# Attention values of two successive chunks in one group of matmuls on four 64x64 quarters of the array, and gate results on two PSUM banks

## The chip, the core and the metric

The kernel runs on one core of one Trainium2 chip. The metric is the device time of one execution in microseconds (us); before the change it is 826.69 us, the median of three runs (826.07 to 826.80). Five engines with instruction queues of their own work side by side: TensorE (PE, matrix products), VectorE (DVE), ScalarE (ACT), GpSimd (POOL) and SyncE (SP, here the queue that loads weights). They hand work over by semaphores. Matmul results go to PSUM, which has eight banks; the kernel uses them as pu0, pu1, pu2, ps0, ps1, pt, po and pc, each 128 partitions by 512 float32.

## The reference

Two layers of a hybrid encoder on 256 positions by 1024 channels, in float32. Per layer:

```
h = rmsnorm(x); proj = h @ w_in            # q | k | v | conv input | gate logits
q, k = rope(q), rope(k)
s = q_chunk . k_band / 8                   # chunks of 64; keys: previous chunk and own
m = max(max(s), sink); p = exp(s - m)
o = (p / (sum(p) + exp(sink - m))) @ v_band
y_attn = o @ w_attn_o
y_conv = silu(layernorm(dwconv31(glu(conv input)))) @ w_conv_o
x += (sigmoid(g_a) * y_attn + sigmoid(g_c) * y_conv) @ w_out
x += (silu(gt) * val) @ w_ffn_down         # gt, val = dwconv3(rmsnorm(x) @ w_ffn_up)
```

There are 16 query heads and 2 key/value heads of 64 channels, so 8 query heads share one key/value head; 4 chunks of 64 positions.

## The kernel before, in words

All activations lie with channels on partitions and the 256 positions along the free dimension. All weights are cut into units of 16 blocks of 128x128 (1 MB). Three slots hold raw weights; for unit u ACT rounds the raw block to a high part (`whi`, line 315) after TensorE has finished the unit that used the slot, GpSimd or VectorE subtracts for the low part (`wlo`, line 253), and TensorE forms each product from three matmuls (high times high, high times low, low times high, lines 1034 to 1036). A unit is 48 such matmuls. Slot and result bank of a unit are both u % 3. Before a unit overwrites its bank it waits until the unit three before it has been read (`result_read`).

Units per layer: 0 to 7 conv input, 8 keys and values, 9 to 12 queries, 13 to 20 gates (`U_GATE`), 21 to 24 attention output (`U_AO`), then conv output, merge output and the feed-forward units.

Attention is woven into the gate units. It has eight groups n (key/value head n // 4, chunk n % 4), each with 8 heads on four pairs. In iteration i TensorE runs gate unit U_GATE+i+1 (in the last iteration instead half of an attention output unit, `group_half(0, 0)`), then `transpose_probs(i)` (line 1157, into bank pt), then `values(i-1)` (line 1168, into the first half of po). Scores of two groups at a time (line 1146) are put into the middle of every second gate unit; they already run as 64x64 matmuls. After the last iteration come `group_half(1, 0)`, `values(7)`, the channel sums of the convolution (`sum_quarters`, line 1064, bank ps0), and `group_half(0, 1)`, which needs all groups. Float32 matmuls such as the transposes, the scores and the values appear as two records for each one in the program.

In `values(n)` the two matmuls have all 128 keys on the rows of the array and 64 of its columns each: even heads go to partitions 0 to 63 of the output, odd heads to 64 to 127. They wait for the copy of the transposed probabilities, and for the reading of the output of the group before (`ol_ready`), as there is one output bank.

ACT in iteration i: copy the transposed probabilities of i-1 (`evict_transposed`, line 478), exponentials of i (`exps`, line 493), high part of the attention output of i-2 (`high_of_o`, line 484, semaphore `oh_ready`), scale the probabilities of i (`probabilities`, line 502), tanh of gate unit i (line 516), `whi` of the unit three later (line 315), and two products for the convolution (line 343). DVE in iteration i: maxima, convolution taps, denominators (lines 808, 812), low part of the attention output of i-2 (`low_of_o`, line 818, semaphore `ol_ready`), more taps. The order on each engine is the written order of the code; no scheduler changes it.

Of the kernel before, what the change touches and what calls it, by code (L numbers as in the profile page):

```python
# [9 lines left out]
P = 128  # L10
# [64 lines left out]
def hybrid_encoder(nc, x_in, pos_in, const_in, par_in, gf_in, w_in, y_out):  # L75
# [3 lines left out]
    with ctx:  # L79
# [62 lines left out]
        outputs = po[:, 0, :].rearrange("p (b t) -> p b t", b=GROUP_PAIRS)  # L142
# [24 lines left out]
        tr_done, pt_ready, pv_done, oh_ready, ol_ready = sem("tr_done"), sem("pt_ready"), sem("pv_done"), sem("oh_ready"), sem("ol_ready")  # L167
        xc_ready, t_ready, silu_ready, uh_ready, ul_ready = sem("xc_ready"), sem("t_ready"), sem("silu_ready"), sem("uh_ready"), sem("ul_ready")
# [17 lines left out]
        def lo_count(s, n):  # L186

            return n + PIECES

# [117 lines left out]
        def _(act):  # L307
# [103 lines left out]
            for l in range(DEPTH):  # L411
# [68 lines left out]
                def high_of_o(n):  # L480

                    c, g = n % N_CHUNKS, n // N_CHUNKS
                    act.wait_ge(pv_done, l * GROUPS + n + 1)
                    A(oh[:, 4 * g:4 * g + 4, CHUNK * c:CHUNK * c + CHUNK], outputs, ACT.Copy).then_inc(oh_ready, 1)
# [20 lines left out]
                for i in range(NT):  # L505
                    u = U_GATE + i
                    if i >= 1:
                        evict_transposed(i - 1)
                    exps(i)
                    if i >= 2:  # L510
                        high_of_o(i - 2)
                    probabilities(i)
                    if i == 4:
                        act.wait_ge(rope_done, l * 10 + 10)
                    act.wait_ge(unit_done[u % RING], finished(l, u))
                    A(gate[:, :, i, :], pu[u % RING][:, :, :], ACT.Tanh, scale=0.5).then_inc(gate_ready, 1)
                    next_high(l, u)
# [24 lines left out]
                for i in range(4):  # L542
                    act.wait_ge(m_step, l * 12 + 4 + 2 * i + 2)
                    A(hh[:, 2 * i:2 * i + 2, :], pu[(U_CO + i) % RING][:, :, :], ACT.Copy, scale=0.5).then_inc(hh_ready, 1)
                    next_high(l, U_CO + i)
                for i in range(4):
                    act.wait_ge(x_ready, l * 8 + i + 1)
                    y = pu[(U_OUT + i) % RING]
# [76 lines left out]
        def _(dve):  # L625
# [94 lines left out]
            for l in range(DEPTH):  # L720
# [93 lines left out]
                def low_of_o(n):  # L814
                    c, g = n % N_CHUNKS, n // N_CHUNKS
                    dve.wait_ge(oh_ready, l * GROUPS + n + 1)
                    at = (slice(0, P), slice(4 * g, 4 * g + 4), slice(CHUNK * c, CHUNK * c + CHUNK))
                    V.tensor_tensor(ol[at], outputs, oh[at].bitcast(f32), ALU.subtract).then_inc(ol_ready, 1)
# [16 lines left out]
                def merge_attention(i):  # L835

                    u = U_AO + i
                    dve.wait_ge(gate_ready, l * NT + NT)
                    dve.wait_ge(unit_done[u % RING], finished(l, u))
                    g0 = gate[:, 0, 2 * i:2 * i + 2, :]  # L840
                    V.scalar_tensor_tensor(g0, g0, 1.0, pu[u % RING][:, :, :], ALU.add, ALU.mult).then_inc(m_step, 1)
# [38 lines left out]
                for i in range(4):  # L880
                    u = U_CO + i
                    dve.wait_ge(unit_done[u % RING], finished(l, u))
                    dve.wait_ge(m_step, l * 12 + 4 + 2 * i)
                    y = pu[u % RING][:, :, :]
# [13 lines left out]
                def input_low(i):  # L898

                    y = pu[(U_OUT + i) % RING]  # L900
# [20 lines left out]
                for i in range(4):  # L921
# [3 lines left out]
                    V.tensor_tensor(pu[u % RING][:, :, :], pu[u % RING][:, :, :], x2, ALU.add).then_inc(x_ready, 1)  # L925
# [9 lines left out]
                    V.tensor_copy(x2, pu[u % RING][:, :, :]).then_inc(x_copied, 1)  # L935
                dve.wait_ge(rstd_ready, l * 3 + 3)

                def scale_up(s, ab, done_value):

                    dve.wait_ge(unit_done[s], done_value)  # L940
                    V.tensor_tensor(up[:, ab, :, :], pu[s][:, :, :], rstd[:, :].unsqueeze(1).to_broadcast([P, 2, T]),  # L941
                                    ALU.mult).then_inc(up_ready, 1)
# [24 lines left out]
                scale_up(0, 0, finished(l, U_FFN))  # L967
                hidden_tile(k0, 0, PA_FW, PA_FW + FT * 4)
                split_low(0, 12)
                scale_up(1, 1, finished(l, U_FFN + 1))  # L970
# [4 lines left out]
                def ffn_step(j, parity, last):  # L975
                    k = j * 2 + l * FT
                    col = j * 8 + PA_FW
                    scale_up(2, 0, l * USES + j + 11)
# [3 lines left out]
                    scale_up(0, 1, l * USES + j + 12)  # L982
# [44 lines left out]
        def _(pe):  # L1027
# [10 lines left out]
            def unit(s, uses_before, hi, lo, ready=None, between={}):  # L1038
# [3 lines left out]
                for m in range(2):  # L1042
                    for k in range(NT):
# [4 lines left out]
                        last = product(pu[s][:, m, :], s, 2 * k + m, hi[:, k, :], lo[:, k, :], k == 0, k == NT - 1)  # L1048
# [28 lines left out]
            def paired_unit(s, hi, lo, before, sums):  # L1077

                for p in range(NT // 2):
                    before(p)  # L1080
                    for k in (2 * p, 2 * p + 1):
                        for m in range(2):
                            last = product(pu[s][:, m, :], s, 2 * k + m, hi[:, k, :], lo[:, k, :], k == 0 and m == 0, k == NT - 1, True)
# [31 lines left out]
            for l in range(DEPTH):  # L1115
                def standard(u, hi, lo, ready=None, between={}):
                    if u >= RING:
                        pe.wait_ge(*result_read(l, u - RING))
                    unit(u % RING, uses(l, u), hi, lo, ready, between)

                def in_pairs(u, hi, lo, ready):
# [4 lines left out]
                    paired_unit(s, hi, lo, ready, {})  # L1126
# [33 lines left out]
                def values(n):  # L1160
                    c, g = n % N_CHUNKS, n // N_CHUNKS
                    pe.wait_ge(v_ready, l * 2 + 2)
                    pe.wait_ge(pt_ready, l * GROUPS + n + 1)
                    if n:
                        pe.wait_ge(ol_ready, l * GROUPS + n)
                    for odd in range(2):
                        rows, queries = slice(64 * odd, 64 * odd + 64), slice(CHUNK * (odd ^ (n % 2)), CHUNK * (odd ^ (n % 2)) + CHUNK)
                        last = MM(outputs[rows, :, :], vwin[:, c, HEAD_DIM * g:HEAD_DIM * g + HEAD_DIM],
                                  probsT[n % 2][:, :, queries], start=True, stop=True)
                    last.then_inc(pv_done, 1)  # L1170
# [22 lines left out]
                else:  # L1193
                    for s in range(UNSCALED):
                        pe.wait_ge(hi_ready[s], hi_count(l * USES))
                        pe.wait_ge(lo_ready[s], lo_count(s, l * USES))
                        paired_unit(s, uh, ul, unscaled_parts, {1: first_total} if s == 1 else {})
# [8 lines left out]
                if l == 0:  # L1206
                    pe.wait_ge(*result_read(l, U_GLU))
                    pe.wait_ge(hi_ready[0], hi_count(1))
                    paired_unit(0, hh, hl, fourth_parts, {})
# [19 lines left out]
                def group_half(i, group):  # L1229

                    s, n = (U_AO + i) % RING, uses(l, U_AO + i)
                    if group == 0:
                        pe.wait_ge(*result_read(l, U_AO + i - RING))
# [3 lines left out]
                        pe.wait_ge(ol_ready, l * GROUPS + N_CHUNKS)  # L1237
# [3 lines left out]
                    for m in range(2):  # L1241
                        for k in range(GROUP_PAIRS * group, GROUP_PAIRS * (group + 1)):
                            last = product(pu[s][:, m, :], s, 2 * k + m, oh[:, k, :], ol[:, k, :],
# [57 lines left out]
                def ffn_step(j, parity):  # L1301
# [3 lines left out]
                    unit(2, n + 10, uh, ul)  # L1305
                    pe.wait_ge(up_ready, k)
                    unit(0, n + 11, uh, ul)
# [97 lines left out]
```

## Time and profile before

| what | value |
|---|---|
| median of 3 runs | 826.69 us |
| the profiled execution, its own time | 827.24 us |
| span of its trace | 825.44 us |
| TensorE busy | 808.1 us, 98% of the span |
| VectorE, ScalarE, GpSimd busy | 71%, 63%, 55% |
| granted TensorE clock | 0.997 of full speed |
| all values matmuls (line 1168) | 64 records, 10.4 us |
| all transposes of probabilities (line 1157) | 64 records, 9.7 us |
| all scores (line 1146) | 256 records, 8.8 and 2.7 us |

A record on TensorE reaches from its start to the modelled end of its results; records overlap, so the cost of a step is read from start to start. A line of the timeline merges neighbouring records of one kind: its second number is the time from the first start to the last end. The iterations described above lie at about 95 to 159 us (first layer) and 496 to 560 us (second layer).

### The profile page before, as it was taken

How to read it: one execution, taken by the hardware profiler on the slowest of the kernel's cores; microseconds unless marked ns; L12 is line 12 of the kernel's file. 1: busy time of each engine (PE TensorE's matmuls, PEld its weight loads, DVE VectorE, ACT ScalarE, POOL GpSimd, SP SyncE). 2: the span in 40 equal slices, each digit the busy share in tenths (PEclk: the TensorE clock that was granted, in tenths of full speed). 3: DMA queues.
4: the chain of work that ended last, by engine and by line, in shares of the span. 5: the costliest groups of instructions: out<-in, count | busy, mean ns of one | idle time of the engine just before them, and what ended most of it. 6: DMA issues, size and time to landing. Idle time of an engine off the chain costs nothing.

```text
span 825.4 us, 16620 instructions
## 1 busy us (share of the span) xinstructions
PE 808.1 (98%) x6820; PEld 790.5 (96%) x6820; DVE 588.8 (71%) x1162; ACT 518.8 (63%) x852; POOL 456.7 (55%) x140
## 2 busy tenths in 40 slices
PE   8999999999999999999999999999999999999996
PEld 7999989899999999999999999989999999999995
DVE  5799998583559766666579999876535887665664
ACT  6856798773665655555576587887446654554543
POOL 6898787687722233222289987887875032223220
PEclk9999999999999999999999999999999999999998
DMA  8654444445455655555455544444454456545521
GB/s 288 212 204 148 161 151 150 154 155 189 169 172 185 205 187 177 199 170 188 154 197 168 198 154 154 154 145 151 165 194 165 157 202 204 202 155 201 179 81 52
DMA packets 21386, 142.26 MB, mean 172 GB/s; under 512 B 2624, under 2 KB 3136, under 8 KB 4672
## 3 DMA queue, kind: packets, MB, share of 16 engines
q1 hardware_dynamic: 20592, 140.43, 49.5%
q8 instruction: 54, 0.88, 0.4%
q10 hardware_dynamic: 720, 0.78, 0.3%
q14 instruction: 20, 0.16, 0.1%
HBM read 140.15 MB, written 1.05 MB: 171 GB/s over the span
## 4 chain that ended last, share of the span: by engine, by line
PE 78%; ACT 9%; DVE 8%; issue 2%; DMA 1%; POOL 1%; SPq 0%; DVEq 0%; ACTq 0%
PE pu L1034 21%; PE pu L1035 20%; PE pu L1036 20%; ACT whi L315 4%; DVE wlo L894 3%; PE ps L1034 2%; PE ps L1036 2%; PE ps L1035 2%; DVE pc L749 2%; ACT qk L563 1%; PE pt L1036 1%; PE pt L1035 1%; PE pt L1034 1%; DMA x<-in_x_t 1%; DVE gate L941 1%
## 5 line engine op out<-in xcount | busy, mean ns | idle before, releaser
L253 POOL TENSOR_TENSOR wlo<-raw,whi 128x2048 fp32r<-128x2048 f32 x86 | 397.3, 4624 | 334.0 <-ACT whi L315 333.8
L1034 PE MATMUL pu<-uh,whi 128*128 128x256 f32 x880 | 249.8, 284 | 1.8 <-POOL wlo L253 1.4
L315 ACT ACTIVATE whi<-raw 128x2048 fp32r<-128x2048 f32 x129 | 245.7, 1906 | 8.3 <-PE pu L1036 7.3
L1035 PE MATMUL pu<-ul,whi 128*128 128x256 f32 x880 | 249.0, 283 | 0.0
L1036 PE MATMUL pu<-uh,wlo 128*128 128x256 f32 x880 | 249.0, 283 | 0.0
L1034 PE MATMUL pu<-hh,whi 128*128 128x256 f32 x704 | 201.6, 286 | 2.2 <-POOL wlo L253 1.4
L1035 PE MATMUL pu<-hl,whi 128*128 128x256 f32 x704 | 199.1, 283 | 0.0
L1036 PE MATMUL pu<-hh,wlo 128*128 128x256 f32 x704 | 199.1, 283 | 0.0
L1034 PEld LDWEIGHTS pu<-uh,whi 128*128 128x128 f32 x880 | 168.9, 192 | 2.4 <-issue 2.3
L1035 PEld LDWEIGHTS pu<-ul,whi 128*128 128x128 f32 x880 | 168.9, 192 | 0.1
L1036 PEld LDWEIGHTS pu<-uh,wlo 128*128 128x128 f32 x880 | 168.9, 192 | 0.0
L749 DVE SCALAR_TENSOR_TENSOR pc<-upad,par_all,pc 128x256 f32<-128x256 f32 x404 | 162.9, 481 | 0.1
L1034 PEld LDWEIGHTS pu<-hh,whi 128*128 128x128 f32 x704 | 134.9, 192 | 8.2 <-issue 7.1
L1035 PEld LDWEIGHTS pu<-hl,whi 128*128 128x128 f32 x704 | 135.0, 192 | 0.0
L1036 PEld LDWEIGHTS pu<-hh,wlo 128*128 128x128 f32 x704 | 135.0, 192 | 0.0
L563 ACT ACTIVATE qk<-gate,par_all 128x256 f32<-128x256 f32 x88 | 48.2, 594 | 124.7 <-DVE gate L941 124.7
L894 DVE TENSOR_TENSOR wlo<-raw,whi 128x2048 fp32r<-128x2048 f32 x42 | 95.9, 2284 | 0.0
L955 DVE SCALAR_TENSOR_TENSOR qk<-gate,par_all,qk 128x254 f32<-128x254 f32 (+1 forms) x176 | 73.3, 478 | 30.0 <-ACT qk L563 30.0
L941 DVE TENSOR_TENSOR gate<-pu,rstd 128x512 f32<-128x512 f32 x44 | 30.2, 687 | 63.9 <-PE pu L1036 57.4
L1034 PE MATMUL ps<-oh,whi 128*128 128x256 f32 x176 | 50.0, 284 | 0.5 <-DVE ol L963 0.5
L1036 PE MATMUL ps<-oh,wlo 128*128 128x256 f32 x176 | 49.8, 283 | 0.0
L1035 PE MATMUL ps<-ol,whi 128*128 128x256 f32 x176 | 49.8, 283 | 0.0
(210 smaller groups left out, 1232.9 us busy)
## 6 DMA issues: line engine op xcount, KB each, us to landing
raw<-in_weights SPq DMA_DIRECT2D x130, 1024.0 KB, 4.9
raw<-in_weights SPq DMA_DIRECT2D x3, 512.0 KB, 8.8
x<-in_x_t SPq DMA_DIRECT2D x2, 256.0 KB, 4.8
raw<-in_weights SPq DMA_DIRECT2D x2, 256.0 KB, 3.9
x<-in_x_t SPq DMA_DIRECT2D x1, 512.0 KB, 8.0
out_y<-qk SPq DMA_DIRECT2D x2, 256.0 KB, 2.8
out_y<-qk ACTq DMA_DIRECT2D x2, 256.0 KB, 2.7
par_all<-in_params SPq DMA_DIRECT2D x1, 236.0 KB, 6.9
```

The lines of the kernel that those rows point to most:

```text
L253: nc.gpsimd.tensor_tensor(wlo[s][:, :], raw[s][:, :], whi[s][:, :].bitcast(f32), ALU.subtract).then_inc(lo_ready[s], 1)
L315: A(whi[s][:, :], raw[s][:, :], ACT.Copy).then_inc(hi_ready[s], 1)
L563: A(fbuf[:, ab, half, :], up[:, ab, half, :], ACT.Identity, scale=par[:, col + 2:col + 2 + 1], bias=par[:, col + 3:col + 3 + 1]).then_inc( ...
L749: V.scalar_tensor_tensor(out, upad[:, t, k:k + T], w, sums, ALU.mult, ALU.add).then_inc(conv_step, 1)
L894: V.tensor_tensor(wlo[s][:, :], raw[s][:, :], whi[s][:, :].bitcast(f32), ALU.subtract).then_inc(lo_ready[s], 1)
L941: V.tensor_tensor(up[:, ab, :, :], pu[s][:, :, :], rstd[:, :].unsqueeze(1).to_broadcast([P, 2, T]), ALU.mult).then_inc(up_ready, 1)
L955: last = V.scalar_tensor_tensor(acc, up[:, ab, half, 0:T - shift], par[:, col:col + 1], acc, ALU.mult, ALU.add).then_inc(f_tap, 1)
L1034: MM(out, whi[s][:, w], hi, start=start, stop=False, skip_group_check=accumulate)
L1035: MM(out, whi[s][:, w], lo, start=False, stop=False, skip_group_check=accumulate)
L1036: return MM(out, wlo[s][:, w], hi, start=False, stop=stop, skip_group_check=accumulate)
```

## The change

- `values` is called for two groups at once, n and n+1, in iterations 2, 4 and 6 (before the transposes of that iteration) and once after the loop. It issues eight matmuls of 64 rows by 64 columns in two turns. In the first turn group n uses one half of the keys and group n+1 the other half, so that four matmuls stand on four quarters; in the second turn the halves are exchanged and the results are added to those of the first. Between the turns TensorE waits for its own semaphore `first_keys`.
- Even groups write po, odd groups pu0 (the last one pu2).
- To free pu0, gate results go to pu1 and pu2 in turn, so a gate unit waits for the reading of the unit two before it. Weight slots stay u % 3. From unit 21 up to the second feed-forward unit the banks are named in the order 1, 0, 2.
- The high and low parts of the attention output lag by three iterations; iteration 7 handles group 4 and 5, the end groups 6 and 7.

```diff
+        def result_bank(u):
+            if U_GATE <= u < U_AO:
+                return 1 + (u - U_GATE) % 2
+            return (1, 0, 2)[u % RING] if U_AO <= u < U_FFN + 2 else u % RING
+        def used_before(u):
+            return u - 2 if U_GATE + 2 <= u <= U_AO else u - RING
...
-                    if i >= 2:
+                    if i >= 3:
+                        high_of_o(i - 3)
+                    if i == GROUPS - 1:
                         high_of_o(i - 2)
...
-                    if i >= 2:
+                    if i >= 3:
+                        low_of_o(i - 3)
+                    if i == GROUPS - 1:
                         low_of_o(i - 2)
...
                 def values(n):
-                    c, g = n % N_CHUNKS, n // N_CHUNKS
+                    g = n // N_CHUNKS
                     pe.wait_ge(v_ready, l * 2 + 2)
-                    pe.wait_ge(pt_ready, l * GROUPS + n + 1)
+                    pe.wait_ge(pt_ready, l * GROUPS + n + 2)
                     if n:
                         pe.wait_ge(ol_ready, l * GROUPS + n)
-                    for odd in range(2):
-                        rows, queries = slice(64 * odd, 64 * odd + 64), slice(CHUNK * (odd ^ (n % 2)), CHUNK * (odd ^ (n % 2)) + CHUNK)
-                        last = MM(outputs[rows, :, :], vwin[:, c, HEAD_DIM * g:HEAD_DIM * g + HEAD_DIM],
-                                  probsT[n % 2][:, :, queries], start=True, stop=True)
-                    last.then_inc(pv_done, 1)
+                    if n == GROUPS - 2:
+                        pe.wait_ge(gate_ready, l * NT + NT)
+                    for turn in range(2):
+                        if turn:
+                            pe.wait_ge(first_keys, l * (GROUPS // 2) + n // 2 + 1)
+                        for m in (n, n + 1):
+                            c = m % N_CHUNKS
+                            keys = slice(64 * (turn ^ (m % 2)), 64 * (turn ^ (m % 2)) + 64)
+                            for odd in range(2):
+                                rows, queries = slice(64 * odd, 64 * odd + 64), slice(CHUNK * (odd ^ (m % 2)), CHUNK * (odd ^ (m % 2)) + CHUNK)
+                                last = MM(outputs(m)[rows, :, :], vwin[keys, c, HEAD_DIM * g:HEAD_DIM * g + HEAD_DIM],
+                                          probsT[m % 2][keys, :, queries], start=(turn == 0), stop=(turn == 1), skip_group_check=True)
+                        last.then_inc(*((pv_done, 2) if turn else (first_keys, 1)))
...
-                        pe.wait_ge(ol_ready, l * GROUPS + N_CHUNKS)
+                        pe.wait_ge(ol_ready, l * GROUPS + N_CHUNKS + 2 * i)
...
+                    if i and i % 2 == 0:
+                        values(i - 2)
                     transpose_probs(i)
-                    if i:
-                        values(i - 1)
                 group_half(1, 0)
-                values(GROUPS - 1)
+                values(GROUPS - 2)
```

On TensorE in iteration 2 of the first layer, before (pt: transposed probabilities, po: attention output, pu: unit results; the number of slot or bank stands behind a name):

```order
L1036 MATMUL pu1<-hh,wlo1 128x256
L1157 MATMUL pt<-const,probs0 128x128 [waits pt_ready,rope_done,p_ready]
L1157 MATMUL pt<-const,probs0 128x128 x3
L1168 MATMUL po<-probsT1,vwin 64x256 [waits ol_ready,pt_ready,v_ready]
L1168 MATMUL po<-probsT1,vwin 64x256
L1034 MATMUL pu2<-hh,whi2 128x256 [waits lo_ready2,hi_ready2,gate_ready]
```

The same place now:

```order
L1054 MATMUL pu2<-hh,wlo1 128x256
L1194 MATMUL po<-probsT0,vwin 64x256 [waits pt_ready,v_ready]
L1194 MATMUL po<-probsT0,vwin 64x256
L1194 MATMUL pu0<-probsT1,vwin 64x256 x2
L1194 MATMUL po<-probsT0,vwin 64x256 [waits first_keys]
L1194 MATMUL po<-probsT0,vwin 64x256
L1194 MATMUL pu0<-probsT1,vwin 64x256 x2
L1175 MATMUL pt<-const,probs0 128x128 [waits pt_ready,rope_done,p_ready]
L1175 MATMUL pt<-const,probs0 128x128 x3
L1052 MATMUL pu1<-hh,whi2 128x256 [waits lo_ready2,hi_ready2,gate_ready]
```

The values of groups 0 and 1 now stand ahead of the transposes of group 2; before, the values of group 0 stood one unit earlier and those of group 1 behind these transposes.

On TensorE after the last iteration, between the two halves of the attention output units, before:

```order
L1036 MATMUL pu1<-oh,wlo1 128x256
L1168 MATMUL po<-probsT1,vwin 64x256 [waits ol_ready,pt_ready,v_ready]
L1168 MATMUL po<-probsT1,vwin 64x256
L1064 MATMUL ps0<-cv,quarter 32x256 [waits conv_step,pool_conv,exp_done]
L1064 MATMUL ps0<-cv,quarter 32x256 x3
L1064 MATMUL ps0<-cv,quarter 32x256 [waits conv_step]
L1064 MATMUL ps0<-cv,quarter 32x256 x3
L1034 MATMUL pu0<-oh,whi0 128x256 [waits ol_ready,oh_ready]
```

The same place now:

```order
L1054 MATMUL pu0<-oh,wlo1 128x256
L1194 MATMUL po<-probsT0,vwin 64x256 [waits ol_ready,gate_ready,pt_ready,v_ready]
L1194 MATMUL po<-probsT0,vwin 64x256
L1194 MATMUL pu2<-probsT1,vwin 64x256 x2
L1194 MATMUL po<-probsT0,vwin 64x256 [waits first_keys]
L1194 MATMUL po<-probsT0,vwin 64x256
L1194 MATMUL pu2<-probsT1,vwin 64x256 x2
L1082 MATMUL ps0<-cv,quarter 32x256 [waits conv_step,pool_conv,exp_done]
L1082 MATMUL ps0<-cv,quarter 32x256 x3
L1082 MATMUL ps0<-cv,quarter 32x256 [waits conv_step]
L1082 MATMUL ps0<-cv,quarter 32x256 x3
L1052 MATMUL pu1<-oh,whi0 128x256 [waits ol_ready,oh_ready]
```

Values of two groups stand here where there was one; before, the values of group 6 stood one half unit earlier.

On ACT in the last iteration and behind it, now (line 492 copies transposed probabilities, 507 are the exponentials, 498 the high part of the attention output, 516 the scaling, 532 the tanh, 380 the copy of the channel sums):

```order
L492 ACTIVATE probsT<-pt 128x512 [waits tr_done]
L505 ACTIVATE mass<-mass 128x4 [waits mx_step]
L507 ACTIVATE probs,mass<-ps,less_top 128x128 x4
L498 ACTIVATE oh<-po 128x4x64 [waits pv_done]
L498 ACTIVATE oh<-pu 128x4x64 [waits pv_done]
L516 ACTIVATE probs<-probs,share 128x128 [waits den_step]
L516 ACTIVATE probs<-probs,share 128x128 x3
L532 ACTIVATE gate<-pu 128x2x256 [waits unit_done2]
L329 ACTIVATE whi<-raw 128x2048 [waits unit_done2,raw_in2]
L492 ACTIVATE probsT<-pt 128x512 [waits tr_done]
L498 ACTIVATE oh<-po 128x4x64 [waits pv_done]
L498 ACTIVATE oh<-pu 128x4x64 [waits pv_done]
```

Before, one high part (of group 5) stood between the exponentials and the scaling; the rest of the row is as it was.

## Rows read from the trace of the kernel before

**Rows 1.** The page: busy time of the engines; the chain that ended last

```profile
PE 808.1 (98%) x6820; PEld 790.5 (96%) x6820; DVE 588.8 (71%) x1162; ACT 518.8 (63%) x852; POOL 456.7 (55%) x140
...
PE 78%; ACT 9%; DVE 8%; issue 2%; DMA 1%; POOL 1%; SPq 0%; DVEq 0%; ACTq 0%
```

**Rows 2.** Timeline of TensorE, iteration 0: start, length, line, operation, [idle before]

```profile
101.73 0.66 PE L1157 MATMUL pt<-const,probs 128*128 128x128 f32 x4 [0.16 <-ACT probs L502]
102.14 0.36 PE L1034 MATMUL pu<-hh,whi 128*128 128x256 f32 x1
102.34 0.28 PE L1035 MATMUL pu<-hl,whi 128*128 128x256 f32 x1
```

**Rows 3.** Timeline of TensorE, iteration 1, with values of group 0

```profile
110.74 0.28 PE L1036 MATMUL pu<-hh,wlo 128*128 128x256 f32 x1
110.86 0.60 PE L1157 MATMUL pt<-const,probs 128*128 128x128 f32 x4
111.39 0.65 PE L1168 MATMUL po<-probsT,vwin 128*64 128x256 f32 x4
111.98 0.38 PE L1034 MATMUL pu<-hh,whi 128*128 128x256 f32 x1
112.20 0.28 PE L1035 MATMUL pu<-hl,whi 128*128 128x256 f32 x1
```

**Rows 4.** Line 1168 on TensorE: shortest, median, longest record in ns

```profile
L1168 PE MATMUL po<-probsT,vwin x64: 379/404/430, 111.4 to 558.4; 128*64 128x256 f32 x64
```

**Rows 5.** Timeline of TensorE, scores on four quarters, in iterations 1 and 3

```profile
106.86 1.10 PE L1146 MATMUL ps<-kr,qk 64*64 64x128 f32 x32 [1.62 <-ACT probs L493]
...
121.80 0.28 PE L1036 MATMUL pu<-hh,wlo 128*128 128x256 f32 x1
122.01 1.10 PE L1146 MATMUL ps<-kr,qk 64*64 64x64 f32 x32
```

**Rows 6.** Timeline of ACT, iterations 0, 2 and 3: tanh, weights, tanh, last exponential

```profile
101.58 0.58 ACT L516 ACTIVATE gate<-pu 128x512 f32<-128x512 f32 x1
102.06 1.90 ACT L315 ACTIVATE whi<-raw 128x2048 fp32r<-128x2048 f32 x1
...
115.40 0.58 ACT L516 ACTIVATE gate<-pu 128x512 f32<-128x512 f32 x1
...
120.34 0.22 ACT L493 ACTIVATION_READ_ACCUMULATOR probs<-ps,less_top 128x1 f32 x1
```

**Rows 7.** Timeline of TensorE, iterations 6 and 7 and the end, first layer

```profile
148.12 0.60 PE L1157 MATMUL pt<-const,probs 128*128 128x128 f32 x4
...
152.82 0.66 PE L1157 MATMUL pt<-const,probs 128*128 128x128 f32 x4 [0.45 <-ACT probs L502]
...
157.05 0.65 PE L1168 MATMUL po<-probsT,vwin 128*64 128x256 f32 x4
157.63 1.07 PE L1064 MATMUL ps<-cv,quarter 128*32 128x256 f32 x16
158.73 0.36 PE L1034 MATMUL pu<-oh,whi 128*128 128x256 f32 x1
```

**Rows 8.** Timeline of ACT, iteration 7 and the end, first layer

```profile
148.99 0.58 ACT L478 ACTIVATE probsT<-pt 128x512 f32<-128x512 f32 x1
...
150.93 0.39 ACT L484 ACTIVATE oh<-po 128x256 fp32r<-128x256 f32 x1
151.49 1.28 ACT L502 ACTIVATE probs<-probs,share 128x128 f32<-128x128 f32 x4 [0.17 <-DVE share L812]
...
157.75 0.38 ACT L484 ACTIVATE oh<-po 128x256 fp32r<-128x256 f32 x1 [1.94 <-PE po L1168]
```

**Rows 9.** Timeline of DVE, the low part of the last group

```profile
158.16 0.42 DVE L818 TENSOR_TENSOR ol<-po,oh 128x256 fp32r<-128x256 f32 x1 [1.90 <-ACT oh L484]
```

**Rows 10.** Timeline of TensorE, the same two places of the second layer

```profile
553.85 0.66 PE L1157 MATMUL pt<-const,probs 128*128 128x128 f32 x4 [0.45 <-ACT probs L502]
...
559.77 0.36 PE L1034 MATMUL pu<-oh,whi 128*128 128x256 f32 x1
```

More of the change, by code:

```diff
@@ L141, in hybrid_encoder, with outputs @@
         fold = [h32[:, n, :] for n in range(2)]
-        outputs = po[:, 0, :].rearrange("p (b t) -> p b t", b=GROUP_PAIRS)
+        def outputs(n):
+            into = po if n % 2 == 0 else pu[2] if n == GROUPS - 1 else pu[0]
+            return into[:, 0, :].rearrange("p (b t) -> p b t", b=GROUP_PAIRS)
         raw_in = [sem(f"raw_in{s}") for s in range(RING)]
@@ L167, in hybrid_encoder @@
         tr_done, pt_ready, pv_done, oh_ready, ol_ready = sem("tr_done"), sem("pt_ready"), sem("pv_done"), sem("oh_ready"), sem("ol_ready")
+        first_keys = sem("first_keys")
         xc_ready, t_ready, silu_ready, uh_ready, ul_ready = sem("xc_ready"), sem("t_ready"), sem("silu_ready"), sem("uh_ready"), sem("ul_ready")
@@ L483, in high_of_o @@
                     act.wait_ge(pv_done, l * GROUPS + n + 1)
-                    A(oh[:, 4 * g:4 * g + 4, CHUNK * c:CHUNK * c + CHUNK], outputs, ACT.Copy).then_inc(oh_ready, 1)
+                    A(oh[:, 4 * g:4 * g + 4, CHUNK * c:CHUNK * c + CHUNK], outputs(n), ACT.Copy).then_inc(oh_ready, 1)
                 def exps(n):
@@ L515, in _ @@
                     act.wait_ge(unit_done[u % RING], finished(l, u))
-                    A(gate[:, :, i, :], pu[u % RING][:, :, :], ACT.Tanh, scale=0.5).then_inc(gate_ready, 1)
+                    A(gate[:, :, i, :], pu[result_bank(u)][:, :, :], ACT.Tanh, scale=0.5).then_inc(gate_ready, 1)
                     next_high(l, u)
@@ L543, in _ @@
                     act.wait_ge(m_step, l * 12 + 4 + 2 * i + 2)
-                    A(hh[:, 2 * i:2 * i + 2, :], pu[(U_CO + i) % RING][:, :, :], ACT.Copy, scale=0.5).then_inc(hh_ready, 1)
+                    A(hh[:, 2 * i:2 * i + 2, :], pu[result_bank(U_CO + i)][:, :, :], ACT.Copy, scale=0.5).then_inc(hh_ready, 1)
                     next_high(l, U_CO + i)
@@ L840, in merge_attention @@
                     g0 = gate[:, 0, 2 * i:2 * i + 2, :]
-                    V.scalar_tensor_tensor(g0, g0, 1.0, pu[u % RING][:, :, :], ALU.add, ALU.mult).then_inc(m_step, 1)
+                    V.scalar_tensor_tensor(g0, g0, 1.0, pu[result_bank(u)][:, :, :], ALU.add, ALU.mult).then_inc(m_step, 1)
                 assert step_now == CONV_STEPS
@@ L924, in _ @@
                     x2 = x[:, 2 * i:2 * i + 2, :]
-                    V.tensor_tensor(pu[u % RING][:, :, :], pu[u % RING][:, :, :], x2, ALU.add).then_inc(x_ready, 1)
+                    V.tensor_tensor(pu[result_bank(u)][:, :, :], pu[result_bank(u)][:, :, :], x2, ALU.add).then_inc(x_ready, 1)
                     if i >= 2:
@@ L1036, in product, with unit @@
                 return MM(out, wlo[s][:, w], hi, start=False, stop=stop, skip_group_check=accumulate)
-            def unit(s, uses_before, hi, lo, ready=None, between={}):
+            def unit(s, into, uses_before, hi, lo, ready=None, between={}):
                 pe.wait_ge(hi_ready[s], hi_count(uses_before))
@@ L1047, in unit @@
                             ready(k // 2)
-                        last = product(pu[s][:, m, :], s, 2 * k + m, hi[:, k, :], lo[:, k, :], k == 0, k == NT - 1)
+                        last = product(pu[into][:, m, :], s, 2 * k + m, hi[:, k, :], lo[:, k, :], k == 0, k == NT - 1)
                 last.then_inc(unit_done[s], 1)
@@ L1075, in _, with paired_unit @@
             pe.wait_ge(setup, 3)
-            def paired_unit(s, hi, lo, before, sums):
+            def paired_unit(s, into, hi, lo, before, sums):
                 for p in range(NT // 2):
@@ L1082, in paired_unit @@
                         for m in range(2):
-                            last = product(pu[s][:, m, :], s, 2 * k + m, hi[:, k, :], lo[:, k, :], k == 0 and m == 0, k == NT - 1, True)
+                            last = product(pu[into][:, m, :], s, 2 * k + m, hi[:, k, :], lo[:, k, :], k == 0 and m == 0, k == NT - 1, True)
                     if p == NT // 2 - 1:
@@ L1117, in standard @@
                     if u >= RING:
-                        pe.wait_ge(*result_read(l, u - RING))
-                    unit(u % RING, uses(l, u), hi, lo, ready, between)
+                        pe.wait_ge(*result_read(l, used_before(u)))
+                    unit(u % RING, result_bank(u), uses(l, u), hi, lo, ready, between)
                 def in_pairs(u, hi, lo, ready):
@@ L1125, in in_pairs @@
                     pe.wait_ge(lo_ready[s], lo_count(s, n))
-                    paired_unit(s, hi, lo, ready, {})
+                    paired_unit(s, result_bank(u), hi, lo, ready, {})
                 def parts_ready(high, high_before, low, low_before):
@@ L1242, in group_half @@
                         for k in range(GROUP_PAIRS * group, GROUP_PAIRS * (group + 1)):
-                            last = product(pu[s][:, m, :], s, 2 * k + m, oh[:, k, :], ol[:, k, :],
+                            last = product(pu[result_bank(U_AO + i)][:, m, :], s, 2 * k + m, oh[:, k, :], ol[:, k, :],
                                            k == 0 and m == 0, k == NT - 1, True)
@@ L1304, in ffn_step @@
                     pe.wait_ge(up_ready, k - 1)
-                    unit(2, n + 10, uh, ul)
+                    unit(2, 2, n + 10, uh, ul)
                     pe.wait_ge(up_ready, k)
-                    unit(0, n + 11, uh, ul)
+                    unit(0, 0, n + 11, uh, ul)
                     pe.wait_ge(hi_ready[1], hi_count(n + 11))
```

28 lines of the change are left out of this document (14 added, 14 removed).

## The prediction

> **What bounds the kernel now.** I read the page first: TensorE is busy for 98% of the span and holds most of the chain that ended last [rows 1]. Whatever is started later or takes longer on TensorE's queue is therefore nearly all paid, and work on ACT and DVE counts only where TensorE waits for it. Next I read TensorE's timeline through the attention iterations. It shows matmul after matmul 0.12 us apart and three places where another engine decides: the scores in iteration 1 of the first layer (idle 1.62 us for the exponentials [rows 5]), the transposes of group 7 (idle 0.45 us for the scaled probabilities [rows 7], again in the second layer [rows 10]), and the half unit at 158.73, which waits for the low part that DVE ends at 158.16 + 0.42 = 158.58 [rows 7, 9]. The last two lie just where the change moves things.
>
> **What one group of values costs now.** Start to start: transposes at 110.86, the second matmul of the next unit at 112.20, so 1.34 us with values [rows 3]. Without values it is 102.34 - 101.73 = 0.61, of which 0.06 is the first transpose, longer there because it had waited (0.66 for 0.60) [rows 2, 3]; so 0.55. One group costs 1.34 - 0.55 = 0.78. Of that 0.58 is the block itself (111.39 to 111.98), the rest is the change from 128x128 to 64-column matmuls and back, 0.10 on either side. Sixteen groups are 12.5 us.
>
> **What a pair will cost.** The records of one group start within 0.65 - 0.38 = 0.27 us, and the last one takes 0.38 until its results stand [rows 3, 4]. Is a quarter matmul cheaper? A float32 record of 128 columns goes through in 0.11 us in the transposes (three further starts in 0.60 - 0.27). The scores are 32 records of 64x128 in 1.10 us [rows 5]: one at a time they would take 3.5 us, in fours 8 x 0.11 plus 0.16 until the last results (a transpose record is 0.60 - 3 x 0.11 = 0.27 long, of which 0.11 is the stream) and a first load of 0.05 (430 less 379 ns [rows 4]), which is 1.10. So four quarters work at once, but each record needs as long as a full one. Half the rows and twice the matmuls then leave the streaming time as it was: two turns of 2 x 0.22 us for a pair, two groups of 2 x 0.22 before. Nothing is won there.
> - First turn: 0.65, plus 0.02 for four quarters instead of two, until its results stand.
> - The wait on `first_keys`: nothing hides it, since the whole queue of TensorE stands behind it. The trace has no wait of TensorE on itself. From below it is a turn that flows on; from above the 0.15 between DVE's end at 158.58 and the matmul at 158.73. TensorE to ACT takes 0.05 (157.05 + 0.65 to 157.75 [rows 7, 8]). I take 0.06, nearest to that single hand-over.
> - Second turn, to the next start: 0.58.
> - Entry from a 128x128 unit: 0.21 (121.80 to 122.01 [rows 5]) instead of 0.12, so 0.09; the first transpose behind it 0.06.
>
> The block is 0.67 + 0.06 + 0.59 = 1.32, the pair 1.47 against 1.56 for two groups. The mode changes saved are nearly eaten by letting the array run empty between the turns.
>
> The Trainium skill, TensorEngine Tiling (Array Packing), section Instruction Overhead, gives each matmul some 60 cycles of overhead, which speaks against twice as many. By its figure the 8 extra records of a pair would add 0.2 us (an estimate at 2.4 GHz), some 1.6 us in all. The scores bear it out only partly: their records start in fours in 0.11 us, the streaming time.
>
> **Two banks for gates.** A gate unit now needs the tanh of the unit two before it. The first to wait is at 102.14, its tanh ends at 101.58 + 0.58 = 102.16 [rows 2, 6]: up to 0.1 us, and free in the first layer, since TensorE idles 1.62 us for ACT afterwards. Later the tanh of iteration 2 ends at 115.98, while its unit starts about 24 x 0.12 before the scores at 122.01, at 118.9: 2.9 us of slack. The exponentials that scores need end at 120.56 [rows 6]; they come 0.6 later (below), the scores 0.1 earlier, and 0.7 us of slack is left. Cost 0.
>
> **Where the path goes, first layer, as shift against before.**
> 1. Transposes of group 6. Before them stood five groups, 3.9 us; now three pairs, 4.4 us. Shift +0.48 at their end. (Each pair stands ahead of the transposes of its iteration, which is also why ACT is late by 0.6 in iterations 3 and 5.)
> 2. Their copy on ACT started at 148.99 though they ended at 148.72, as ACT was busy. It now starts at 148.72 + 0.48 + 0.06 = 149.27: +0.28.
> 3. Between exponentials and scaling stand two high parts instead of one. The second costs about 0.30 to the next start (0.38, less the 0.09 by which ACT records overlap, 102.06 against 102.16 [rows 6]); of the 0.56 from 150.93 to 151.49, 0.17 was a wait for DVE [rows 8], which it covers, and 0.60 now stands for 0.56. Scaling, and with it the transposes of group 7: +0.32. TensorE idles for it as before, longer.
> 4. The values of group 6 are gone from behind them: -0.78, shift -0.46 at the last values. The copy of group 7 is ready by then: tanh, weights and copy after the scaling end by 156, the pair starts at 156.6.
> 5. Pair instead of one group: 1.32 against 0.58, shift +0.28 at the channel sums.
> 6. The half unit behind waits for two high parts in a row on ACT before the last low part: +0.30. Shift +0.58.
>
> Behind that point order and durations are unchanged and TensorE leads, so nothing gives it back. The second layer shows the same idle time before the transposes of group 7, and from them to the half unit 5.92 us against 5.91 [rows 7, 10], so the same sum is taken for it. Two layers: +1.2 us. GpSimd, DMA and later bank names: 0; their work starts from the same units, shifted by less than a microsecond.
>
> The profiled execution is 827.24 (span 825.44 and 1.8 around it), so it would be 828.4; it lies 0.55 above the median of 826.69. From the median: 827.8 us.
>
> **Rivals.**
> - *The turns flow on without running empty.* For it: a second turn needs only weights and data that are long there. Against: weight loads of the second turn stand behind the wait. A pair is then 0.28 cheaper (0.23 of wait and latency, 0.05 of first load): 1.19. Transposes of group 6 shift by -0.35, ACT by -0.6 to -0.5, and each layer ends near -0.6: 825.5 us.
> - *Slower by the starts.* Not the stream but the start of each quarter matmul decides. The 32 records of the scores allow up to 1.10 / 32 = 0.034 us each [rows 5]; 8 more in each pair are 0.27, counted four times a layer (three ahead of group 6, one at the end): +2.2, 830.0 us. Decisive if four quarters with 256 columns start more than 0.22 us after the four before.
> - *Slower, since the two row halves take turns.* Values of both halves are read and added in two banks; if only two quarters ran at once, a pair would take four blocks of streaming, +0.85, four times a layer: +6.8, 834.6 us. Against: 1.10 us for the scores. It decides from the point where the first turn lasts over 0.9 us.
> - *The end is not longer.* If the second high part and the third pair hide in ACT's slack (steps 2, 3 and 6 nothing), each layer is at about 0: 826.7 us.
>
> **How the numbers follow.** Main case 0.68, own range 827.0 to 828.7 (wait of 0 to 0.15 beyond the results; steps 3 and 6 half or full). Flowing turns 0.13; starts 0.07; row halves 0.05; no longer end 0.07. A measurement here tells 0.2%, or 1.65 us, from no change: below 825.04 is faster, above 828.34 slower. Main case 0.53 same, 0.15 slower; flowing turns 0.06 same, 0.07 faster; starts and row halves 0.12 slower; the last 0.07 same. Together faster 0.07, same 0.66, slower 0.27. The range for 8 in 10 takes in most of the flowing and of the starts case: 825.5 to 830.0.
>
> **What would show it.** Right: the first turn's records start within 0.28 us, the second turn starts 0.45 us after the last of the first, and a block lasts 1.3 us; the transposes of group 7 start 0.3 us later against a fixed point of the layer, with some 1.1 us of idle before them (0.45, 0.32 for ACT, 0.30 since the values of group 5 no longer lie between); the half unit after the channel sums waits for DVE's low part about 0.3 us longer. Wrong: a block near 1.1 or above 1.6 us, a gate unit that waits for a tanh for more than 0.2 us in many iterations, or a TensorE wait on GpSimd that was not there.

## The result, and the profile after

The changed kernel takes 828.19 us (median of 11 runs, 827.83 to 829.79) against 826.59 us for the kernel before (11 runs, 826.07 to 827.15): ratio 1.0021, 95% interval 1.0013 to 1.0029. The forecast was 827.8 us, "same" at 0.66, with 828.34 as the edge to slower. It is slower by 1.6 us, and the interval lies clear of no change; the median stays under the edge, so it counts as "same".

The page of the profiled execution (828.07 us, span 826.3) answers to [rows 1]; TensorE's busy time is even a little less than before, and the granted clock is 0.998 of full speed against 0.997, so the clock is not behind the difference:

```profile
PE 807.4 (98%) x6884; PEld 791.0 (96%) x6884; DVE 588.7 (71%) x1162; ACT 518.9 (63%) x852; POOL 456.7 (55%) x140
```

The list of TensorE's waits (line that waited, line it waited for, total us, times, longest) shows where time went. The second line was 1.1 us in total before; the waits for `ol L834` (DVE's low part of the attention output) were not there:

```profile
PE pu L1052 <- POOL wlo L267: 2.9, 3, 1.4
PE pt L1175 <- ACT probs L516: 2.2, 3, 1.0
PE ps L1164 <- ACT probs L507: 1.5, 1, 1.5
...
PE pu L1052 <- DVE ol L834: 0.8, 2, 0.4
```

Two groups of values in eight matmuls are called a pair here; its block is the time from its first start to the start of the next kind of matmul. Now the first pair on TensorE's timeline (start, length, line), which answers to [rows 3]:

```profile
116.32 0.28 PE L1054 MATMUL pu<-hh,wlo 128*128 128x256 f32 x1
116.53 0.43 PE L1194 MATMUL po<-probsT,vwin 64*64 64x256 f32 x2
116.54 0.43 PE L1194 MATMUL pu<-probsT,vwin 64*64 64x256 f32 x2
116.79 0.38 PE L1194 MATMUL po<-probsT,vwin 64*64 64x256 f32 x2
116.81 0.38 PE L1194 MATMUL pu<-probsT,vwin 64*64 64x256 f32 x2
117.28 0.43 PE L1194 MATMUL po<-probsT,vwin 64*64 64x256 f32 x2
117.29 0.43 PE L1194 MATMUL pu<-probsT,vwin 64*64 64x256 f32 x2
117.54 0.38 PE L1194 MATMUL po<-probsT,vwin 64*64 64x256 f32 x2
117.56 0.38 PE L1194 MATMUL pu<-probsT,vwin 64*64 64x256 f32 x2
117.87 0.66 PE L1175 MATMUL pt<-const,probs 128*128 128x128 f32 x4
```

Four quarters start within 0.02 us, their second records 0.26 later; then nothing starts until 117.28, because the second turn waits for the first turn's results, which the profile puts at 116.81 + 0.38 = 117.19 (the ends of matmuls are modelled there, the starts are not). The block from 116.53 to 117.87 is 1.34 us for two groups, where one group took 0.58.

TensorE at the end of the first layer's attention part, answering to [rows 7]:

```profile
148.03 0.66 PE L1175 MATMUL pt<-const,probs 128*128 128x128 f32 x4
...
152.59 0.66 PE L1175 MATMUL pt<-const,probs 128*128 128x128 f32 x4 [1.04 <-ACT probs L516]
...
157.39 1.07 PE L1082 MATMUL ps<-cv,quarter 128*32 128x256 f32 x16
158.84 0.36 PE L1052 MATMUL pu<-oh,whi 128*128 128x256 f32 x1 [0.38 <-DVE ol L834]
```

and ACT at the same places, answering to [rows 8]:

```profile
148.72 0.60 ACT L492 ACTIVATE probsT<-pt 128x512 f32<-128x512 f32 x1 [0.39 <-PE pt L1175]
...
150.69 0.40 ACT L498 ACTIVATE oh<-po 128x256 fp32r<-128x256 f32 x1
150.95 0.41 ACT L498 ACTIVATE oh<-pu 128x256 fp32r<-128x256 f32 x1
151.25 1.28 ACT L516 ACTIVATE probs<-probs,share 128x128 f32<-128x128 f32 x4
...
157.53 0.38 ACT L498 ACTIVATE oh<-po 128x256 fp32r<-128x256 f32 x1 [2.23 <-PE pu L1194]
157.81 0.38 ACT L498 ACTIVATE oh<-pu 128x256 fp32r<-128x256 f32 x1
```

The low part of the last group on DVE, answering to [rows 9], ends at 158.28 + 0.41 = 158.69, and the half unit starts at 158.84:

```profile
158.28 0.41 DVE L834 TENSOR_TENSOR ol<-pu,oh 128x256 fp32r<-128x256 f32 x1
```

Two executions differ in how early the first inputs are there (here 0.63 us, to the other side; over all profiled runs the same scores start between 105.54 and 106.86), so starts are best compared from a fixed point of each layer. I take the start of the scores in iteration 1, which stand ahead of the first pair: 106.86 and 507.89 before, 106.23 and 508.01 after.

```profile
106.23 1.10 PE L1164 MATMUL ps<-kr,qk 64*64 64x128 f32 x32 [1.52 <-ACT probs L507]
```

From there, in us (first layer; the second agrees within 0.03 in these two kernels and in all of the experiments but the last):

| kernel | transposes of group 6 | transposes of group 7 | channel sums | half unit behind the sums |
|---|---|---|---|---|
| before | 41.26 | 45.96 | 50.77 | 51.87 |
| changed | 41.80 | 46.36 | 51.16 | 52.61 |

A layer is 0.74 us longer at the half unit (0.72 in the second); 1.46 us in all, of the 1.6 measured. Behind that point the starts run in step again: 229.12 against 229.01 for the same matmul at the head of the second feed-forward unit, which is 0.63 earlier at the fixed point and 0.74 later since.

### The profile page after: what moved, and what is told of

Same layout as the page of the kernel before. It is cut to its first block, busy times and chain, and to the rows that moved or that the text cites. A ratio compares the mean times of both kernels' runs of the same rounds, so it can differ in the third digit from the quotient of the medians.

```text
span 826.3 us, 16742 instructions
## 1 busy us (share of the span) xinstructions
PE 807.4 (98%) x6884; PEld 791.0 (96%) x6884; DVE 588.7 (71%) x1162; ACT 518.9 (63%) x852; POOL 456.7 (55%) x140
## 4 chain that ended last, share of the span: by engine, by line
PE 79%; DVE 8%; ACT 8%; issue 2%; DMA 1%; POOL 1%; SPq 0%; DVEq 0%; ACTq 0%
PE pu L1052 21%; PE pu L1054 21%; PE pu L1053 21%; ACT whi L329 3%; DVE wlo L912 3%; PE ps L1052 2%; PE ps L1053 2%; PE ps L1054 2%; DVE pc L765 2%; PE po L1194 1%; ACT qk L579 1%; PE pt L1054 1%; PE pt L1053 1%; PE pt L1052 1%; PE pt L1175 1%
```

## The experiments

They were timed in two sessions, each beside the kernel before on the same chip (before: 826.37 us in the session of the first four, 826.24 in that of the last three). Each kernel ran 11 times, the last one 5 times. The table gathers what came out; the last two columns are starts from the fixed point as above, the half unit being the one behind the channel sums.

| kernel | median us | ratio to before, 95% interval | block | transposes 7 | half unit |
|---|---|---|---|---|---|
| full rows, one turn | 825.09 | 0.9984 (0.9975 to 0.9993) | 1.015 | 45.37 | 51.28 |
| banks only | 826.20 | 0.9998 (0.9989 to 1.0007) | 0.582 (one group) | 45.98 | 51.90 |
| turns flow on | 825.93 | 0.9994 (0.9986 to 1.0003) | 1.025 | 45.41 | 51.36 |
| other end | 827.39 | 1.0013 (1.0004 to 1.0021) | 1.343 | 46.34 | 52.33 |
| full rows and other end | 824.54 | 0.9979 (0.9970 to 0.9987) | 1.015 | 45.38 | 51.03 |
| and third buffer | 824.30 | 0.9976 (0.9967 to 0.9985) | 1.014 | 45.27 | 50.92 |
| and late products | 823.60 | 0.9966 (0.9954 to 0.9979) | 1.014 | 44.41 | 50.58 |

### Full rows, one turn

```diff
-                    for turn in range(2):
-                        if turn:
-                            pe.wait_ge(first_keys, ...)
-                        for m in (n, n + 1):
...
+                    for m in (n, n + 1):
+                        c = m % N_CHUNKS
+                        for odd in range(2):
+                            rows, queries = ...
+                            last = MM(outputs(m)[rows, :, :], vwin[:, c, HEAD_DIM * g:HEAD_DIM * g + HEAD_DIM],
+                                      probsT[m % 2][:, :, queries], start=True, stop=True)
+                    last.then_inc(pv_done, 2)
```

> The changed kernel with one thing undone: the values of a pair run in one turn as four matmuls of 128 rows by 64 columns (group n into po, group n+1 into the second bank), with no halves of the keys and no wait on first_keys; pairing, order and gate banks stay. If the price is the emptying of the array between the turns and quarters win nothing in streaming, a block takes 1.00 us from its first start to the next kind of matmul (0.27 + 2 x 0.21 + 0.31) instead of 1.34, the transposes of group 7 come 0.65 earlier than in the kernel before (ACT leads there), and the half unit behind the channel sums 0.6 to 0.7 earlier: two layers -1.3, some 825.3 us, 0.16% below before and 2.9 us below the changed kernel. If pairing itself (later copies, two high parts in a row) is what costs, it stays at or above 826.6 us.

TensorE's timeline at the first pair:

```profile
115.83 0.65 PE L1190 MATMUL po<-probsT,vwin 128*64 128x256 f32 x4
116.31 0.60 PE L1190 MATMUL pu<-probsT,vwin 128*64 128x256 f32 x4
116.84 0.66 PE L1175 MATMUL pt<-const,probs 128*128 128x128 f32 x4
```

The second group starts 0.48 us after the first, with nothing between. The block is 1.01 us instead of 1.34, the time 825.09, where 825.3 was expected. Undoing the quarters, and with them the wait between the turns, turns a loss of 1.6 us into a gain of 1.3 against before. So pairing is worth something, and the quarters with their wait cost more than it. The other theory, that pairing itself is the loss, falls.

### Banks only

```diff
-            into = po if n % 2 == 0 else pu[2] if n == GROUPS - 1 else pu[0]
+            into = po
...
-                    if i and i % 2 == 0:
-                        values(i - 2)
                     transpose_probs(i)
+                    if i:
+                        values(i - 1)
```

`values`, the high and low parts and the end are those of the kernel before.

> The kernel before with the bank part alone: gate results on pu1 and pu2 in turn, banks 1, 0, 2 behind; values one group at a time as before. If two banks are enough for the gates, nothing moves: 826.6 us, TensorE's starts through the attention iterations as before within 0.1 us, apart from at most 0.1 us at the gate unit of iteration 1, which the idle time before the scores takes up. If the narrower banks are behind the part of the loss that was not forecast (0.15 us a layer), it shows 0.15 us or more a layer by the first transposes of group 7.

The transposes of group 7 wait as they did:

```profile
152.39 0.66 PE L1171 MATMUL pt<-const,probs 128*128 128x128 f32 x4 [0.46 <-ACT probs L516]
```

From the fixed point on, starts agree with the kernel before within 0.03 us. Two banks are enough for the gates; the 0.16 us a layer that the forecast missed is not here.

### Turns flow on

```diff
-                        if turn:
-                            pe.wait_ge(first_keys, ...)
...
-                                last = MM(outputs(m)[rows, :, :], ..., start=(turn == 0), stop=(turn == 1), skip_group_check=True)
-                        last.then_inc(*((pv_done, 2) if turn else (first_keys, 1)))
+                                last = MM(outputs(m ^ turn, turn)[rows, :, :], ..., start=True, stop=True)
+                    last.then_inc(pv_done, 2)
```

`outputs(n, half)` takes the second half of the bank where `half` is 1.

> The changed kernel with the second turn written to the second halves of the same two banks, each bank by the same half of the rows as in the first turn, so that TensorE needs no wait between the turns. The addition of the second turn's results is left out, so part of the attention output is missing. Everything else is as in the changed kernel. If the wait costs what the trace shows (0.46 us from the last start of the first turn to the second turn, against 0.21 in a flow, and a first load of 0.05), a block takes 1.04 us and the time is near 825.6 us (-1.0 against before). If quarters have a cost of their own besides the wait, the block stays above 1.15 us.

```profile
116.48 0.43 PE L1192 MATMUL po<-probsT,vwin 64*64 64x256 f32 x2
116.49 0.43 PE L1192 MATMUL pu<-probsT,vwin 64*64 64x256 f32 x2
116.74 0.38 PE L1192 MATMUL po<-probsT,vwin 64*64 64x256 f32 x2
116.76 0.38 PE L1192 MATMUL pu<-probsT,vwin 64*64 64x256 f32 x2
116.96 0.38 PE L1192 MATMUL po<-probsT,vwin 64*64 64x256 f32 x2
116.97 0.38 PE L1192 MATMUL pu<-probsT,vwin 64*64 64x256 f32 x2
117.18 0.38 PE L1192 MATMUL po<-probsT,vwin 64*64 64x256 f32 x2
117.19 0.38 PE L1192 MATMUL pu<-probsT,vwin 64*64 64x256 f32 x2
117.50 0.66 PE L1175 MATMUL pt<-const,probs 128*128 128x128 f32 x4
```

Without the wait the second set of four starts 0.26 us after the first, as in the changed kernel, and each further set follows after 0.22 us; the block is 1.025 us. The wait thus costs 1.343 - 1.025 = 0.318 us a pair, and quarters as such cost 0.010 over full rows. In the trace the half unit comes 0.51 and 0.53 earlier than before in the two layers; the timed runs show less of it (-0.4 us, interval from -1.2 to +0.2). Part of that difference lies outside the kernel's instructions: the median span of these executions is 823.7 us against 824.6 before, 0.9 less, but in six of the eleven 2.2 to 2.5 us passed outside the span instead of the usual 1.8. No run shows why. The price of the wait rests on the traces. Part of the result is left out here, so this is not a version to use: the second halves would have to be added afterwards.

### Other end

```diff
+                    if i == GROUPS - 1:
+                        evict_transposed(i)
                     next_high(l, u)
-                evict_transposed(GROUPS - 1)
...
                     for m in range(2):
+                        if m and (i, group) == (1, 0):
+                            values(GROUPS - 2)
...
                 group_half(1, 0)
-                values(GROUPS - 2)
```

> The changed kernel with another end of the attention part: ACT copies the transposed probabilities of group 7 before the weights instead of after, and the last pair stands in the middle of the half unit behind the transposes of group 7, so the high and low parts of groups 6 and 7 lie beside its second half. If the idle time before the last half unit (0.38 us in the trace of the changed kernel) is the two high parts in a row, it is gone, the channel sums come 0.3 later for one more change of mode, and each layer is 0.2 to 0.3 us shorter: about 827.7 us. If the half unit waits there for something else, the idle time stays.

```profile
157.12 0.28 PE L1055 MATMUL pu<-oh,wlo 128*128 128x256 f32 x1
157.33 1.07 PE L1083 MATMUL ps<-cv,quarter 128*32 128x256 f32 x16
158.33 0.39 PE L1053 MATMUL pu<-oh,whi 128*128 128x256 f32 x1
```

The half unit behind the sums now follows them without idle time (0.31 us from the last of them instead of 0.76), the sums stand 0.17 later for the further change of mode, and a layer is 0.28 shorter than in the changed kernel. So the idle time was the two high parts in a row on ACT, with DVE behind them: it is gone once they lie beside matmuls.

### Full rows and other end

The two edits above together.

> The two edits that each helped, together: pairs in one turn on all 128 rows, and the other end (copy of group 7 ahead of the weights, last pair in the middle of the half unit). The first took 0.60 us out of each layer against the kernel before, the second 0.27 against the changed kernel. If they add up, each layer is 0.87 shorter than before: 1.7 us, some 824.7 us. If the wait of the transposes of group 7 for ACT (1.2 us idle) takes back what is won behind it, the sum is smaller; it should not, as that wait lies ahead of both.

They add up: 824.54 us, and the half unit 0.84 and 0.87 us earlier than before in the two layers, where 0.87 was expected. The idle time ahead of the transposes of group 7 stays at 1.04 us, untouched by either:

```profile
151.27 0.66 PE L1176 MATMUL pt<-const,probs 128*128 128x128 f32 x4 [1.04 <-ACT probs L516]
```

### Third buffer

On top of the version before; the copy and the values matmuls take the buffer by `n % 3` and `m % 3`.

```diff
-        probsT = [sb(f"probsT{i}", [P, GROUP_PAIRS, P]) for i in range(2)]
+        probsT = [sb(f"probsT{i}", [P, GROUP_PAIRS, P]) for i in range(3)]
...
-                    if i and i % 2 == 0:
-                        values(i - 2)
                     transpose_probs(i)
+                    if i and i % 2 == 0:
+                        values(i - 2)
```

> The same with a third buffer for the transposed probabilities, so that the transposes of iterations 2, 4 and 6 can stand ahead of the pair again. If ACT's copy in iteration 7 is late because the third pair stands ahead of the transposes of group 6, ACT is now bound by its own work instead and gains 0.16 us only (its copy starts 0.8 instead of 0.6 us earlier than in the kernel before): each layer 0.16 us shorter, 824.4 us. If TensorE's pace and not ACT decides there, nothing changes.

The transposes of group 6 come 1.01 us earlier than in the version without the buffer, those of group 7 only 0.11. On ACT the copy of group 6 no longer waits; it follows the convolution products at once:

```profile
145.98 1.29 ACT L357 ACTIVATE qk<-upad,par_all 128x256 f32<-128x256 f32 x3
147.18 0.58 ACT L492 ACTIVATE probsT<-pt 128x512 f32<-128x512 f32 x1
```

The time moved from 824.54 to 824.30 us with overlapping intervals; the starts show 0.11 and 0.09 us in the two layers where 0.16 was expected.

### Late products

On top of the version with the third buffer:

```diff
-                if u + RING in PRODUCT_UNITS:
+                if u + RING in PRODUCT_UNITS[:-1]:
...
-                    if n == PRODUCTS - 3:
-                        tap_product(l, n + 2)
...
                     probabilities(i)
+                    if i == GROUPS - 1:
+                        tap_product(l, PRODUCTS - 2)
+                        tap_product(l, PRODUCTS - 1)
...
-                        if m and (i, group) == (1, 0):
-                            values(GROUPS - 2)
...
+                            if (m, k, i, group) == (1, 2, 1, 0):
+                                values(GROUPS - 2)
```

> The same, and ACT forms the last three convolution products (1.3 us) behind the scaling of group 7 instead of ahead of its copy, with the last pair three quarters into the half unit. If ACT's chain from the copy of group 6 to the scaling of group 7 is what TensorE idles for ahead of the transposes of group 7 (1.2 us), the idle time nearly goes, these transposes come 1.0 us earlier, and GpSimd's low parts for the next half unit (ready 45.0 us after the first scores of iteration 1) leave a wait of 0.2: 0.8 us a layer, 822.8 us. If something else holds TensorE there, the idle time stays.

The idle time ahead of the transposes nearly goes, and they come 0.87 us earlier. They start 0.21 us behind the last matmul of the unit, where 0.12 is the step between matmuls in a stream; the 0.09 left is still ACT's, whose scaling ends at 148.92 + 1.28 = 150.20:

```profile
148.92 1.28 ACT L514 ACTIVATE probs<-probs,share 128x128 f32<-128x128 f32 x4
```

```profile
150.04 0.28 PE L1056 MATMUL pu<-oh,wlo 128*128 128x256 f32 x1
150.25 0.66 PE L1177 MATMUL pt<-const,probs 128*128 128x128 f32 x4
151.19 0.36 PE L1054 MATMUL pu<-oh,whi 128*128 128x256 f32 x1 [0.28 <-issue]
```

A new wait takes about half of the gain: the half unit right behind these transposes starts 0.94 us after them instead of 0.41 (0.83 in the second layer). Before it GpSimd writes low parts until 146.27 + 4.62 = 150.89:

```profile
146.27 4.62 POOL L267 TENSOR_TENSOR wlo<-raw,whi 128x2048 fp32r<-128x2048 f32 x1 [2.38 <-ACT whi L329]
```

"Issue" names no releaser. That GpSimd is the one is read from the end of its record, 0.30 us before the start here and 0.21 in the second layer; no run leaves it out. The layers gain 0.34 and 0.46 us instead of 0.8, so 822.8 us was missed; at 823.6 us this version is 0.34% below the kernel before (interval 0.21% to 0.46%), and the fastest of all.

## Why the prediction was right

- **Streaming wins nothing.** Right. A pair streams as long on quarters as on full rows: blocks of 1.025 and 1.015 us.
- **The pair.** Forecast 1.47 us, block 1.32. The block is 1.343. From the transposes of group 5, which come 34.17 instead of 34.30 us after the fixed point with two pairs for four groups of 0.78 ahead, a pair is (4 x 0.777 - 0.13) / 2 = 1.49. The hand-over within TensorE was taken at 0.06 and is 0.09 (results at 117.19, next start at 117.28). Each pair was so 0.02 short, four times a layer: half of the 0.16 that the sum missed.
- **The wait.** Forecast 0.23 of wait and 0.05 of first load; measured 0.318 by leaving it out, of which 0.05 is the first load (the second records start 0.266 us after the first ones and not 0.216). The Trainium skill, TensorE: Matmul & The Clock Gate, section Single matmul latency, puts some 166 ns over its streaming time on a single bf16 matmul of the full array at full clock. The trace has about the same for a float32 quarter: 0.376 us of record for 0.216 of stream. The rest of the wait is the hand-over, 0.09, and 0.02 for the four quarters that start one after the other.
- **Step 1 and 2.** Forecast shift of the end of the transposes of group 6 0.48, measured 0.60 (0.54 at the start, and a first transpose 0.06 longer). By the forecast's own terms, 3 x 1.47 - 5 x 0.78, it should have read 0.51. ACT's copy then waits 0.39 for them and starts 0.36 later instead of 0.28.
- **Step 3.** Forecast +0.04, measured 2.53 us from copy to scaling against 2.50 [rows 8]: +0.03. The size is partly luck. From the first high part to the scaling it is 0.56 us both times, as the second high part is wholly covered by the wait for DVE; the 0.03 lies ahead of them, in the copy and the exponentials.
- **Steps 4 to 6.** Transposes of group 7 to channel sums: 4.80 against 4.81 us, forecast -0.04. Sums to half unit: 1.45 against 1.10, +0.35, forecast 0.30.
- **The sum.** +0.74 a layer where +0.58 was forecast, with the same places and signs: 1.46 us by the traces instead of 1.2. Of the 0.16 missed, 0.08 had arisen by the transposes of group 7 (0.06 of it the three pairs ahead, which reach it because ACT now waits for TensorE), 0.03 came with the last pair up to the channel sums, and 0.05 lies in step 6.
- **Gate banks.** Forecast 0; the kernel with this part alone shows 0.03 us at most behind the fixed point. The wait of up to 0.1 us that the forecast allowed the gate unit of iteration 1 in the first layer shows: its second matmul comes 0.70 us after the start of the transposes of iteration 0 instead of 0.61. TensorE then idles 1.52 us for the exponentials instead of 1.62, so it costs nothing.
- **What would show it.** The signs named for right are there: the records of the first turn start within 0.29 us, the second turn starts 0.46 us after the last of them, the transposes of group 7 come 0.40 us later with 1.04 us of idle time ahead, and the half unit idles 0.38 us for DVE.
- **The rivals.** "Flowing turns" is what the kernel would be without the wait; the experiment with it ended at 825.93 us, rival 825.5. "Starts" fell: eight more records a pair cost 0.010 us, a thousandth of a microsecond each, not 0.034. The 60 cycles a matmul of the Trainium skill (TensorEngine Tiling (Array Packing), section Instruction Overhead), added for each record, don't show either: by them the block without the wait would have been 1.2 us (an estimate), and it is 1.025. "Row halves take turns" fell with the first pair: its second turn starts 0.75 us after its first, and the rival asked for over 0.9. "The end is not longer" fell with the idle time of 0.38 us.

The chance of slower was 0.27 and that of same 0.66. The median lies 0.15 us under the edge between them, and the ratio's interval spans it; that it came out as "same" and not as "slower" is partly luck.

## What to carry to other kernels

Look first at what lies idle. Where all 128 rows are in use, as here, cutting a float32 matmul into quarters halves the work of each and doubles their number, and the streaming time stays (blocks of 1.025 and 1.015 us). If the halves have to be added in one bank, a wait within TensorE's own queue comes on top (0.318 us a pair), and nothing hid it here. Putting small steps of two groups together did pay (0.6 us a layer with full rows), as TensorE then enters and leaves the 64-column matmuls once for two groups. Look then for who now gets two items at once at the end of the chain (ACT and DVE here), and put other matmuls beside them.

## What the runs showed of the hardware

A wait of TensorE on its own semaphore cost 0.318 us from stream to stream: 0.16 from the end of a record's stream to its results as the profile models them, 0.02 for the stagger of four quarters, 0.09 to the next start, 0.05 for a weight load that nothing covered. Four 64x64 float32 matmuls of 256 columns start 7 ns apart, and the next four follow after 0.216 us, as two 128x64 matmuls do after 0.21.

Entering 64-column or 64x64 matmuls from 128x128 cost 0.09 us to the first start (0.21 for 0.12) and 0.05 at the second record. Leaving them cost 0.09 to 0.10 to the next start (0.31 behind the last start instead of 0.21 to 0.22), and 0.10 more at the second matmul of a unit or 0.06 at the second transpose.
